# Expert down products with a 64-token stationary operand in two column tiles

## What is computed

```
logits = (t @ w_router);  top_val, top_idx = lax.top_k(logits, 2);  top_w = softmax(top_val)
combine = sum(one_hot(top_idx, 8) * top_w[..., None], axis=1)
y = zeros_like(t)
for e in range(8):
    gt, up = split(t @ w_gate_up[e])          # [1024, 2 x 3584]
    y = y + combine[:, e:e+1] * ((silu(gt) * up) @ w_down[e])   # [3584, 1024]
```

## Time and profile before

| | |
|---|---|
| median of 3 executions | 1546.23 us |
| lowest, highest | 1545.79, 1547.57 us |
| span of the profiled execution | 1544.4 us |
| own time of the profiled execution | not listed; the median of the others is 1.8 us above its span |
| mean granted clock of TensorE | 0.994 of full speed |
| TensorE busy | 1500.5 us (97%) |
| weight loads busy | 937.8 us (61%) |
| VectorE, ScalarE, GpSimd busy | 36%, 28%, 5% |
| mean DMA rate | 311 GB/s over the span |

### The profile page before, as it was taken

One profiled execution on the slowest core, in us unless ns is written; L12 is line 12 of the kernel. 1 busy time (PEld: TensorE's weight loads), 2 busy tenths in 40 slices (PEclk: granted clock), 3 DMA queues, 4 the chain that ended last, 5 costly groups with the idle time before them and its releaser, 6 DMA issues.

```text
span 1544.4 us, 30813 instructions
## 1 busy us (share of the span) xinstructions
PE 1500.5 (97%) x13934; PEld 937.8 (61%) x13934; DVE 555.6 (36%) x672; ACT 430.9 (28%) x551; POOL 83.0 (5%) x126
## 2 busy tenths in 40 slices
PE   8999999999999999999999999999999999998877
PEld 7788888788888887887335353353433533534224
DVE  5755576655567655666400101011010110010101
ACT  6557654544445567554000000000000000000000
POOL 5211100000002111001000000000000000000000
PEclk9999999999999999999999999999999999999999
DMA  7555454665665555678999999999999999999996
GB/s 275 178 152 166 148 166 152 229 188 175 204 189 183 177 147 155 213 291 313 418 398 405 420 426 430 428 427 428 428 427 430 429 426 428 426 431 427 428 428 252
DMA packets 86242, 480.38 MB, mean 311 GB/s; under 512 B 11296, under 2 KB 13408, under 8 KB 64096
## 3 DMA queue, kind: packets, MB, share of 16 engines
q1 hardware_dynamic: 84480, 474.67, 79.3%
q0 software_dynamic: 1632, 3.74, 0.8%
HBM read 477.34 MB, written 1.05 MB: 310 GB/s over the span
## 4 chain that ended last, share of the span: by engine, by line
PE 84%; DMA 11%; DVE 2%; POOL 2%; issue 1%; ACT 0%; SPq 0%; DVEq 0%; POOLq 0%
PE pa L2128 26%; PE ps L2128 18%; PE pa L1998 13%; PE pa L2000 12%; PE pa L1999 12%; DMA exp_raw<-in_moe_slabs 11%; DVE w_lo L1292 1%; DMA w_raw<-in_w_mem_kv 1%; POOL hrs L805 1%; POOL head_gains L734 0%; PE ps L1914 0%; PE ps L2301 0%; PE ps L2122 0%; PE pa L2033 0%; PE ps L2278 0%
## 5 line engine op out<-in xcount | busy, mean ns | idle before, releaser
L2128 PE MATMUL pa<-exp_raw,xf 128*32 128x512 f32 (+1 forms) x5104 | 492.1, 542 | 19.5 <-DMA exp_raw<-in_moe_slabs 17.0
L2128 PEld LDWEIGHTS pa<-exp_raw,xf 128*32 128x32 f32 x5104 | 163.7, 110 | 325.7 <-issue 267.1
L1292 DVE TENSOR_TENSOR w_lo<-w_raw,w_hi 128x1024 fp32r<-128x1024 f32 x226 | 274.2, 1232 | 121.8 <-ACT w_hi L930 112.9
L930 ACT ACTIVATE w_hi<-w_raw 128x1024 fp32r<-128x1024 f32 (+1 forms) x228 | 236.9, 1053 | 146.3 <-PE pa L2000 144.8
L2128 PE MATMUL ps<-exp_raw,hf 128*32 128x256 f32 x4384 | 246.0, 383 | 10.0 <-DMA exp_raw<-in_moe_slabs 8.4
L1998 PE MATMUL pa<-w_hi,r 128*128 128x512 f32 x600 | 239.8, 400 | 1.2 <-DVE r L1327 1.1
L2000 PE MATMUL pa<-w_hi,r 128*128 128x512 f32 x600 | 233.9, 390 | 0.0
L1999 PE MATMUL pa<-w_lo,r 128*128 128x512 f32 x600 | 233.9, 390 | 0.0
L1859 DVE TENSOR_TENSOR hs<-pa,hs 128x768 f32<-128x768 f32 (+3 forms) x32 | 23.7, 742 | 584.2 <-ACT hs L1255 584.2
L2128 PEld LDWEIGHTS ps<-exp_raw,hf 128*32 128x32 f32 x4384 | 144.5, 111 | 114.6 <-issue 13.0
L1255 ACT ACTIVATE hs<-pa 128x768 f32<-128x768 f32 (+3 forms) x32 | 20.4, 637 | 661.0 <-PE pa L2128 661.0
(11 more groups left out here) (280 smaller groups left out, 816.3 us busy)
## 6 DMA issues: line engine op xcount, KB each, us to landing
exp_raw<-in_moe_slabs SPq DMA_DIRECT2D x82, 3072.0 KB, 33.0
exp_raw<-in_moe_slabs SPq DMA_DIRECT2D x87, 1024.0 KB, 8.2
w_raw<-in_w_in SPq DMA_DIRECT2D x104, 512.0 KB, 4.4
w_raw<-in_ff_w_gate_up SPq DMA_DIRECT2D x44, 512.0 KB, 4.5
w_raw<-in_ff_w_down SPq DMA_DIRECT2D x22, 512.0 KB, 4.2
w_raw<-in_w_mem_kv SPq DMA_DIRECT2D x16, 512.0 KB, 5.3
w_raw<-in_w_out SPq DMA_DIRECT2D x16, 512.0 KB, 4.2
w_raw<-in_w_br_sb SPq DMA_DIRECT2D x8, 512.0 KB, 3.7
```

What stands on the lines that cost most here:

```text
L930: act.activation(dst, raw, ACT.Copy).then_inc(hi_ready, 1)
L1292: dve.tensor_tensor(dst, raw, hi.bitcast(F32), ALU.subtract)\
L2128: return pe.matmul(dst, a, b, start=start, stop=stop, skip_group_check=True)
```

## The change

The down product takes the first two blocks of a slot as one stationary operand of 64 tokens, in two column tiles of 64 columns (`half_rows`), each with 512 outputs. A third block, where there is one, follows for the same k tile as before, in four tiles of 32 columns. The hidden activations are laid out so that the blocks of a k tile stand side by side. The scatter takes the first two blocks from 64 partitions at once and the third from 32, and the selection matrix `selT`, its row numbers and its making by VectorE follow (one operation fewer for each slot). The last scatter does the same.

```diff
+PAIR, HALVES = 2 * LANE, 2
-        selT = sb("selT", [P, WIDE_BLOCKS, SEQ], F32R)
+        selT = sb("selT", [P, 2, SEQ], F32R)
...
         def gate_up(s, h, blocks):
             w = lanes_wide(s)
-            return pa[:, 0:blocks * BW].rearrange("p (b c) -> p b c", c=BW)[:, :, h * w:(h + 1) * w]
+            return pa[:, 0:blocks * BW].rearrange("p (b c) -> p b c", c=BW)[:, :, h * w:(h + 1) * w]\
+                .rearrange("p b (k c) -> p b k c", c=LANE)
         def hidden_rows(s, blocks):
             w = lanes_wide(s)
-            return hs[:, 0:blocks * w].rearrange("p (b c) -> p b c", c=w)
+            return hs[:, 0:blocks * w].rearrange("p (k b c) -> p b k c", b=blocks, c=LANE)
+        def half_rows(a, h):
+            return a[h * PAIR:(h + 1) * PAIR]
...
             for g in range(LANES):
-                link(pool.iota(lane(row_no, g), pattern=[[LANE, WIDE_BLOCKS]], base=1,
+                link(pool.iota(lane(row_no, g), pattern=[[PAIR - g % 2 * LANE, 2]],
+                               base=1 + g % 2 * LANE,
...
             def choose(i, blocks):
                 dve.wait_ge(selt_turned, i + 1)
-                for b in range(blocks):
+                for b in range(blocks - 1):
...
             def scatter_slot(n, blocks):
                 for t in range(NT):
-                    for b in range(blocks):
-                        for part in range(2):
-                            for g in range(LANES):
-                                c = g * BW + t * OUT
-                                ins = mm(ps[:, c:c + OUT],
-                                         lane(selT, g)[:, b, t * P:(t + 1) * P],
-                                         lane(yf, g)[:, part, b * OUT:(b + 1) * OUT], ...)
+                    cols, at = slice(t * P, (t + 1) * P), t * OUT
+                    for part in range(2):
+                        for g in (0, 2, 1, 3):
+                            n = g % 2 * OUT
+                            ins = mm(ps[:, g * BW + at:g * BW + at + OUT],
+                                     half_rows(selT, g // 2)[:, 0, cols],
+                                     half_rows(yf, g // 2)[:, part, n:n + OUT], ...)
+                    for part in range(2 if blocks > 2 else 0):
+                        for g in range(LANES):
+                            ins = mm(ps[:, g * BW + at:g * BW + at + OUT],
+                                     lane(selT, g)[:, 1, cols],
+                                     lane(yf, g)[:, part, BW:BW + OUT], False, part == 1)
             def scatter_last(t, bank):
-                for b in range(FEW_BLOCKS):
-                    for g in range(LANES):
-                        ins = mm(bank[:, g * BW:g * BW + OUT], ...)
+                for h in range(HALVES):
+                    ins = mm(bank[:, h * BW:(h + 1) * BW],
+                             half_rows(selT, h)[:, 0, t * P:(t + 1) * P].bitcast(F32),
+                             half_rows(hs, h)[:, 0:BW], True, True)
...
                         for kk in range(n):
                             k = q * n + kk
-                            for b in range(blocks):
-                                for g in range(LANES):
-                                    c = kk * DM + g * OUT
-                                    ins = mm(lane(ps, g)[:, b * OUT:(b + 1) * OUT],
-                                             hf[:, s % 2, (b * chunks + k) * LANE:
-                                                (b * chunks + k + 1) * LANE],
-                                             exp_slots[place(i, j)][:, c:c + OUT], ...)
+                            at = k * blocks * LANE
+                            hidden = hf[:, s % 2, at:at + blocks * LANE]
+                            for h in range(HALVES):
+                                c = kk * DM + h * BW
+                                ins = mm(half_rows(ps, h)[:, 0:BW], hidden[:, 0:PAIR],
+                                         exp_slots[place(i, j)][:, c:c + BW], first, last)
+                            if blocks == 2:
+                                continue
+                            for g in range(LANES):
+                                c = kk * DM + g * OUT
+                                ins = mm(lane(ps, g)[:, BW:BW + OUT], hidden[:, PAIR:],
+                                         exp_slots[place(i, j)][:, c:c + OUT], first, last)
                         ins.then_inc(slab_used, 1)
```

More of the change, by code:

```diff
@@ L313, in trunk @@
         mk, mtmp = sm(496, SLOTS, E), sm(608, SLOTS, E)
-        pos_now, row_no = small[:, 744:744 + NT], small[:, 748:748 + WIDE_BLOCKS]
+        pos_now, row_no = small[:, 744:744 + NT], small[:, 748:750]
         iota_e, rank_of_slot, order = sm(720, E), sm(728, E), sm(736, OVER)
@@ L411, in lanes_wide @@
             return STEP[s][1] // LANES
-        def hidden_chunks(s):
-            return lanes_wide(s) // LANE
         def gate_up(s, h, blocks):
             w = lanes_wide(s)
-            return pa[:, 0:blocks * BW].rearrange("p (b c) -> p b c", c=BW)[:, :, h * w:(h + 1) * w]
+            return pa[:, 0:blocks * BW].rearrange("p (b c) -> p b c", c=BW)[:, :, h * w:(h + 1) * w]\
+                .rearrange("p b (k c) -> p b k c", c=LANE)
         def hidden_rows(s, blocks):
             w = lanes_wide(s)
-            return hs[:, 0:blocks * w].rearrange("p (b c) -> p b c", c=w)
+            return hs[:, 0:blocks * w].rearrange("p (k b c) -> p b k c", b=blocks, c=LANE)
+        def half_rows(a, h):
+            return a[h * PAIR:(h + 1) * PAIR]
         def lane(a, g):
@@ L1880, in _ @@
                 dve.wait_ge(tail_scattered, t + 1)
-                dve.scalar_tensor_tensor(out=xs_lane[:, t],
-                                         in0=bank[:, :].rearrange("p (g c) -> p g c", g=LANES)
-                                         [:, :, 0:OUT],
+                dve.scalar_tensor_tensor(out=xs[:, t, :], in0=bank[:, 0:DM],
                                          scalar=slot_comb[:, t, column(slots)],
-                                         in1=xs_lane[:, t], op0=ALU.mult, op1=ALU.add)\
+                                         in1=xs[:, t, :], op0=ALU.mult, op1=ALU.add)\
                     .then_inc(added, 1)
@@ L2362, in scatter_slot @@
                 for t in range(NT):
-                    for b in range(blocks):
-                        for part in range(2):
-                            for g in range(LANES):
-                                c = g * BW + t * OUT
-                                ins = mm(ps[:, c:c + OUT],
-                                         lane(selT, g)[:, b, t * P:(t + 1) * P],
-                                         lane(yf, g)[:, part, b * OUT:(b + 1) * OUT],
-                                         b == 0 and part == 0 and t == 0,
-                                         b == blocks - 1 and part == 1)
+                    cols, at = slice(t * P, (t + 1) * P), t * OUT
[4 more added lines that the diff above has]
+                                     half_rows(selT, g // 2)[:, 0, cols],
+                                     half_rows(yf, g // 2)[:, part, n:n + OUT],
+                                     part == 0 and t == 0, part == 1 and blocks == 2)
+                    for part in range(2 if blocks > 2 else 0):
[3 more added lines that the diff above has]
+                                     lane(yf, g)[:, part, BW:BW + OUT], False, part == 1)
                 ins.then_inc(scattered, 1)
             def scatter_last(t, bank):
-                for b in range(FEW_BLOCKS):
-                    for g in range(LANES):
[L2378 to L2381, removed]
+                for h in range(HALVES):
+                    ins = mm(bank[:, h * BW:(h + 1) * BW],
+                             half_rows(selT, h)[:, 0, t * P:(t + 1) * P].bitcast(F32),
+                             half_rows(hs, h)[:, 0:BW], True, True)
                 return ins
@@ L2421, in down @@
                     pe.wait_ge(e_turned, i * STEPS + (s + 1))
-                    chunks = hidden_chunks(s)
                     n = EXP_SLAB // DM
@@ L2427, in down @@
                             k = q * n + kk
-                            for b in range(blocks):
-                                for g in range(LANES):
-                                    c = kk * DM + g * OUT
-                                    ins = mm(lane(ps, g)[:, b * OUT:(b + 1) * OUT],
-                                             hf[:, s % 2, (b * chunks + k) * LANE:
-                                                (b * chunks + k + 1) * LANE],
-                                             exp_slots[place(i, j)][:, c:c + OUT],
-                                             s == 0 and k == 0 and b * OUT % BW == 0,
-                                             s == STEPS - 1 and k == HT_END - 1)
+                            first, last = s == 0 and k == 0, s == STEPS - 1 and k == HT_END - 1
+                            at = k * blocks * LANE
[10 more added lines that the diff above has]
```

(1 more changed line is left out.)

## The result

| | before | after |
|---|---|---|
| median of 5 executions | 1546.77 us | 1558.91 us (1557.80 to 1559.08) |
| span of the profiled execution | 1544.4 us | 1556.3 us |
| own time of the profiled execution | not listed | 1558.91 us |
| mean granted clock | 0.994 | 0.998 |

A forecast was written before the change was run, and what follows sets the result against it. The slab stream was taken to set the end, following TensorE in slot 0. Losses of 7.5 us (slot 0) and 6.6 us (slot 5) move the 1544.4 us span by 14.1; runs lie 1.8 above: 1560.3 us, range 1551 to 1571.

The forecast's parts named there:

- Bound: Expert stage: the stream of slabs sets the pace from slot 2 on; in slot 0 the stream follows TensorE.
- Price of a k tile: Down product of three-block slots: changing from 32 to 64 columns and back costs 0.282 us per k tile.
- x = 7.9 us: TensorE's added time in a three-block slot: the k tile's price times 28.
- gap and first load: At each shape change: a 0.105 us gap, plus an open first stationary load, 0.025 us (32 columns) or 0.051 us (64).
- A small term left out: Down product of two-block slots: forecast as 0.1 us for 28 k tiles, counted as nothing.
- Scatter: Scatter after a three-block slot: three more shape changes, near 0.55 us; slot 5's covered by a 0.84 us wait.
- Slot 0: No slack here: TensorE ends 7.9 us late and all later loads are 7.5 us late.
- Slot 2: TensorE's lateness against the stream reaches 8.9 us; the queue is 14.5 us deep, floor not yet reached.
- floor: Queue depth below which the stream runs dry: one load's own time, by estimate 11.2 us.
- Slot 5: Queue at its end falls to 4.6 us, under its floor by 6.6 us; the stream stands still for so long.
- Waits: Slots 6 and 7: about 6 to 9 us of TensorE's waits for slabs are left.
- The idle time takes it: Rival, chance 0.10: 25.4 us of later waits absorb TensorE's 33.2 us of added work, leaving 7.8 us: 1554.0 us.

The follow-up runs named there:

- e1_pairs_two: Changed kernel, but pairs of 64 tokens only in two-block slots; three-block slots keep the loops of before: 1544.38 us, ratio 0.9984 to the kernel before.
- e2_mixed_slot0: Changed kernel, but among the three-block slots only slot 0 mixes 64 and 32 columns: 1551.78 us, ratio 1.0035 to the kernel before.
- e4_mixed_slots45: Changed kernel, but among the three-block slots only slots 4 and 5 mix 64 and 32 columns: 1545.45 us, ratio 0.9991 to the kernel before.
- e6_per_slab: Changed kernel, but each slab takes first both k tiles' pairs, then both third blocks: 1545.95 us, ratio 0.9994 to the kernel before.
- e7_per_part: Changed kernel, but a whole stretch of down slabs goes first as pairs, then third blocks, freeing slabs in the second pass: 1547.63 us, ratio 1.0006.
- e8_mixed_245: Changed kernel, but slot 0 keeps three blocks of 32; slots 2, 4 and 5 mix: 1549.96 us, ratio 1.0018 to the kernel before.
- e9_fetch: Single dose: 2688 small GpSimd writes added to e1_pairs_two: 1546.24 us, ratio 0.9995 to the kernel before.
- e10_fetch_twice: Double dose: 5376 small GpSimd writes added to e1_pairs_two: 1644.65 us, with GpSimd itself running until 1640 us.

## Why the prediction was right, and where it was off

**Bound.** Right. The stream sets the end, but for slot 0, where it follows TensorE; slot 0 and slot 2 alone show it.

**Price of a k tile.** Forecast 0.282 us, x = 7.9 us for a slot. Slot 0 now runs from 739.4 to 858.3 us; it ran from 739.5 to 850.4 us before, as its timeline has it: 7.9 us. The two terms, gap and first load, came from other pairs of shapes and held for 32 and 64 columns. The kernel with half the changes pays half, 0.14 us a change. The Trainium skill has it in TensorEngine Tiling (Array Packing), Key Properties, that a change of the tiling mode drains TensorE. The trace agrees, with 0.14 us a change between 32 and 64 columns on the same 128 rows.

**A small term left out.** I had counted the down product of two-block slots at nothing. It too changes shape, from gate to down and back: the stretch takes 7.02 us and took 6.90 us, 0.12 us more at its end, and about as much falls ahead of its start. Slot 1, with three stretches and no waits, took 77.4 us and now takes 78.7 us (its first matmuls and those of slot 2, before, then changed). That is 1.3 us more, where the forecast had 0.55 for the scatter alone. In slots 6 and 7 TensorE waits anyway.

```profile
850.44 13.92 PE L2128 MATMUL pa<-exp_raw,xf 128*32 128x512 f32 x128
927.86 20.78 PE L2128 MATMUL pa<-exp_raw,xf 128*32 128x512 f32 x192
...
858.30 13.92 PE L2129 MATMUL pa<-exp_raw,xf 128*32 128x512 f32 x128
937.00 20.81 PE L2129 MATMUL pa<-exp_raw,xf 128*32 128x512 f32 x192
```

**Scatter.** Forecast +0.55 us; 874.36 - 872.15 = 2.21 us against 1.63 us, +0.58. For slot 5 I had the price covered by the 0.84 us wait for `hs` of the earlier trace rows, but that row is from slot 4. The wait in slot 5 was shorter, and 0.15 us of the price is left (2.21 us from scatter to gate now, 1261.63 - 1259.57 = 2.06 before):

```profile
1261.63 5.36 PE L2128 MATMUL pa<-exp_raw,xf 128*32 128x512 f32 x48 [0.36 <-DVE hs L1859]
```

**Slot 0.** Forecast 7.5 us lost by the stream, measured 7.1; time to landing fell to 5.5 us and not 6.3.

**Slot 2.** The queue was forecast to be 14.5 us deep at its end and was 11.5 us, already at the floor of 11.2; the rate fell to 415 GB/s there.

**Slot 5, the term that was mis-sized.** I let the stream run at full rate until the time to landing was 11.2 us. The floor was right, 10.7 to 12.5 us in the trace; but the rate falls from 15 us on, and by bytes the stream lost 11.6 us and not 6.6. The last section has the likely reason: a load lands in sixteen parts, and the time to landing counts to the last of them. Near 1240 us the first part came 10 us ahead of it in the kernel before and 6 us ahead in the changed one, so the parts that are ahead run dry sooner. By the last part of each load, which is what TensorE waits for, the changed kernel is 5.9 us behind the kernel before after slot 0, 3.7 us from 1260 to 1290 us, and about 12 us from 1400 us to the end. In these terms slot 5 cost 8.5 us and 2.2 us came back ahead of it, none at the end.

Against the run with pairs alone the drains cost 14.5 us, the forecast had 14.1; and the changed kernel has again 0.18 MB less to fetch than that run. Against the kernel before it is 12.1 us. So the near agreement of the end is partly luck: too little in slot 5, and nothing for the parts that draw together or for the fetches.

**Waits.** Forecast 6 to 9 us left in slots 6 and 7; 9.8 us.

**The idle time takes it.** This rival (1554.0 us) fell with slot 0 alone: 25 us of idle time in later slots did not take 8 us there.

## What to carry to other kernels

Mixing tile shapes inside the inner loop costs a gap and an open weight load at each change, here 0.14 us, and it buys nothing where the columns streamed stay the same; group the work of one shape, but not past the point where buffers are freed late. To price added work on an engine beside a saturated stream, keep a ledger of the queue's depth stretch by stretch: where the queue is empty each microsecond costs about one (7.4 us for 7.9 in slot 0), elsewhere none until the queue has run down. Time to landing is the depth for the slowest part of a load; the quickest parts had 6 to 10 us less here near 1240 us. Pairs where they need no mixing are worth keeping: 1544.4 us, 0.16% under the kernel before.

## What the runs showed of the hardware that was not expected

**Instruction fetches delay a saturated stream by more than their bytes.** 0.17 MB more of fetches cost 1.9 us, and 0.17 MB at 428 GB/s are 0.4 us. In the windows above one of 16 engines moves 26 GB/s. Between 850 and 1535 us the double dose has 37 packets of GpSimd's queue (8 KB, 0.31 us each) more than the run with pairs alone, 12.1 us of one engine's time. The landings, taken up below, show what became of it: of the sixteen parts of the last slab one lands 13.4 us after the fifteenth (1.5 us with pairs alone), and 11.2 us later than the last one of the kernel before, while the mean of the sixteen moves by only 0.8 us. That the additional fetches lay on one engine is inferred from this match; no packet in the traces names its engine. It can't hold for every queue: in the kernel before, the 68 packets of q8 from 850 to 1535 us took 73 us of an engine's time, and no part is that far behind. Nor do the doses add. In the single dose the sixteenth part was 5.7 us after the fifteenth at 1241 us, when the writes had just ended, but only 1.1 us at the last slab. How 1.9 us come of that stays open.

**The stream ends raggedly.** Windows of the kernel before, then of the changed kernel:

```profile
1515.00:1520.00 5.00, 5.00 (x84) 2.90 (x80) 0.00 (x0) 0.00 (x0) 0.00 (x0) 0.86 0.97 400
1520.00:1525.00 5.00, 5.00 (x98) 2.99 (x92) 0.00 (x0) 0.00 (x0) 0.00 (x0) 1.00 0.54 226
1525.00:1530.00 5.00, 5.00 (x100) 3.02 (x96) 1.47 (x3) 0.38 (x1) 0.00 (x0) 1.00 0.51 206
1530.00:1535.00 5.00, 5.00 (x100) 3.02 (x96) 0.00 (x0) 0.00 (x0) 0.00 (x0) 1.00 0.31 123
```

```profile
1527.00:1532.00 5.00, 4.92 (x74) 2.28 (x74) 0.00 (x0) 0.00 (x0) 0.00 (x0) 1.00 0.97 406
1532.00:1537.00 5.00, 5.00 (x96) 2.86 (x88) 0.00 (x0) 0.00 (x0) 0.00 (x0) 1.00 1.01 416
1537.00:1542.00 5.00, 5.00 (x28) 1.72 (x26) 1.46 (x3) 0.38 (x1) 0.00 (x0) 1.00 1.01 421
1542.00:1547.00 5.00, 4.49 (x22) 1.26 (x20) 0.00 (x0) 0.00 (x0) 0.00 (x0) 1.00 0.40 165
```

Before, half of the engines' time is unused from 1520 us on while slabs are still outstanding; the changed kernel keeps all 16 busy until 1542 us. Each load of slabs has sixteen landing records in the traces, as many as the core has DMA engines. I take each for the part that one engine brings. First come the times from the first to the last of the sixteen (us; load nearest to the time named), then for the last slab how far its last part is behind the mean of the sixteen:

```
                    850   1240   1380   last slab   behind the mean
before              2.8   10.0   13.1      14.8          7.4
changed             0.9    5.6    1.5       3.3          2.1
e1_pairs_two        4.0    9.5   12.6      14.1          7.7
e2_mixed_slot0      1.1    8.8   10.9      13.4          7.1
e4_mixed_slots45    2.2    8.2    1.1       3.4          2.0
e6_per_slab         2.0    7.5    4.6       7.7          4.7
e7_per_part         0.6    6.5    9.6      11.1          5.9
e8_mixed_245        2.8    7.6    2.7       5.8          4.4
e9_fetch            2.8   14.7   14.7      14.7          7.5
e10_fetch_twice     1.9   15.6   20.5      25.9         17.9
```

The parts drift apart as long as the queue is deep: from about 2 us to 15 us in 680 us in the kernel before, whose last slab has eight parts landed by 1522.3 us and the other eight from 1532.6 us on. Where the stream runs down they come together again, to about 1 us in slot 0 (changed, slot 0 alone, one change for a stretch) and in slot 5 (changed, slots 4 and 5, slots 2, 4 and 5, and in part one change for a slab); where it doesn't, they don't. After a stop in slot 0 they have 680 us to drift apart again, so the run with slot 0 alone gets back 0.4 us between 1500 us and the end, and one change for a stretch 1.8 us; the kernels with a stop in slot 5 get back 3 to 6 us. So a stop late in a saturated stream is partly free: the mean of the last slab's landings moves by 17.4 us in the changed kernel, and its last part, for which TensorE waits, by 12.0. Why the parts drift apart stays open.
